# Expert weights in 2 MB transfers, two contraction chunks to a transfer, in a hybrid decoder step on one Trainium2 core

## What is computed

```python
def expert_block(args):
    xb, e = args                       # 128 rows of tokens, the number of an expert
    hgu = xb @ w_gu[e] + b_gu[e]       # w_gu[e]: 1024 x 2048
    gate = jnp.minimum(hgu[:, :D_FF], SWIGLU_LIMIT)
    up = jnp.clip(hgu[:, D_FF:], -SWIGLU_LIMIT, SWIGLU_LIMIT)
    act = (up + 1.0) * gate * jax.nn.sigmoid(SWIGLU_ALPHA * gate)
    return act @ w_down[e] + b_down[e] # w_down[e]: 1024 x 1024
```

## Time and profile before

| | |
|---|---|
| median of 3 runs | 1454.49 us (1453.26 to 1455.03) |
| profiled execution | 1456.36 us, its span 1454.6 us |
| PE busy | 1357.5 us, 93% of the span |
| PE clock granted, whole span | 0.944 |
| DMA moved | 438.82 MB, mean 302 GB/s |
| the 32 blocks of experts | 455.5 us to 1402.2 us |

### The profile page before, as it was taken

One profiled execution on the slowest core, in us unless ns is written; L12 is line 12 of the kernel. 1 busy time (PEld: TensorE's weight loads), 2 busy tenths in 40 slices (PEclk: granted clock), 3 DMA queues, 4 the chain that ended last, 5 costly groups with the idle time before them and its releaser, 6 DMA issues.

```text
span 1454.6 us, 17291 instructions
## 1 busy us (share of the span) xinstructions
PE 1357.5 (93%) x6116; PEld 591.3 (41%) x6116; DVE 506.7 (35%) x1073; ACT 202.2 (14%) x385; POOL 52.4 (4%) x103
## 2 busy tenths in 40 slices
PE   6989995598689999999999999999999999999997
PEld 5765884463443333333333333333333333333332
DVE  2673334525445332233223322232223322332223
ACT  2450010000021111111111111111111111111111
POOL 5100010000020000000000000000000000000000
PEclk8999996687569999999999999999999999999999
DMA  8221104002346999999999999999999999999941
GB/s 253 94 84 58 59 3 176 11 0 83 105 147 247 408 422 422 422 422 422 422 422 422 422 422 422 422 422 422 422 422 422 422 422 422 422 422 422 422 176 36
DMA packets 83620, 438.82 MB, mean 302 GB/s; under 512 B 15114, under 2 KB 22423, under 8 KB 34410
## 3 DMA queue, kind: packets, MB, share of 16 engines
q1 hardware_dynamic: 83594, 438.47, 74.2%
HBM read 433.41 MB, written 5.02 MB: 301 GB/s over the span
## 4 chain that ended last, share of the span: by engine, by line
PE 88%; DVE 6%; issue 1%; DMA 1%; ACT 1%; SPq 1%; POOL 0%; POOLq 0%; DVEq 0%; ACTq 0%
PE bank L936 32%; PE bank L946 15%; PE bank L926 7%; PE bank L900 6%; PE bank L570 5%; PE bank L956 3%; PE bank L696 2%; PE bank L1035 2%; PE bank L568 1%; PE bank L908 1%; DVE SC L1366 1%; PE bank L916 1%; PE bank L648 1%; DMA SC<-in_ple_w 1%; PE bank L841 1%
## 5 line engine op out<-in xcount | busy, mean ns | idle before, releaser
L936 PE MATMUL bank<-ring,SC 128*64 128x512 f32 x2048 | 479.1, 600 | 0.7 <-ACT SC L1225 0.7
L936 PEld LDWEIGHTS bank<-ring,SC 128*64 128x64 f32 x2048 | 133.2, 136 | 282.2 <-issue 277.5
L946 PE MATMUL bank<-ring,SC 128*64 128x512 f32 x1024 | 226.8, 595 | 0.0
L1708 DVE TENSOR_TENSOR SC<-bank,bgu 128x256 f32<-128x256 f32 x128 | 48.1, 418 | 437.1 <-PE bank L956 437.1
L1700 DVE TENSOR_TENSOR X<-X,bank 128x512 f32<-128x512 f32 x180 | 115.2, 680 | 97.1 <-PE bank L926 97.1
L946 PEld LDWEIGHTS bank<-ring,SC 128*64 128x64 f32 x1024 | 70.7, 137 | 133.3 <-issue 133.3
L570 PE MATMUL bank<-xT,ring 128*128 128x320 f32 x384 | 109.3, 440 | 0.0
L926 PE MATMUL bank<-SC 64*128 64x512 f32 x360 | 101.6, 641 | 0.0
L900 PE MATMUL bank<-XS,SC 128*64 128x512 f32 x396 | 90.6, 592 | 0.7 <-ACT va L1211 0.7
L570 PEld LDWEIGHTS bank<-xT,ring 128*128 128x128 f32 x384 | 73.1, 194 | 29.7 <-issue 2.4
L1221 ACT ACTIVATE SC<-bank 128x512 f32<-128x512 f32 x33 | 19.7, 598 | 407.0 <-PE bank L900 407.0
(11 more groups left out here) (415 smaller groups left out, 1066.3 us busy)
## 6 DMA issues: line engine op xcount, KB each, us to landing
ring<-in_expert_w_gu SPq DMA_DIRECT2D x256, 1024.0 KB, 15.7
ring<-in_expert_w_down SPq DMA_DIRECT2D x128, 1024.0 KB, 16.4
ring<-in_w_in SPq DMA_DIRECT2D x7, 2048.0 KB, 8.5
ring<-in_w_out SPq DMA_DIRECT2D x1, 4096.0 KB, 14.6
ring<-in_ple_gate_w SPq DMA_DIRECT2D x4, 1024.0 KB, 12.2
out_gdn_s<-ring SPq DMA_DIRECT2D x1, 2048.0 KB, 8.7
X<-in_x_prompt SPq DMA_DIRECT2D x2, 512.0 KB, 3.8
out_c_s<-ring SPq DMA_DIRECT2D x1, 1024.0 KB, 5.9
```

Source lines behind the costliest of these rows:

```text
L936: last = mm(PB[j][SL * h:SL * h + SL, :], xg[:, c % 4, c // 4, :], w[:, FF * h + 512 * j:FF * h + 512 * j + 512], start=(c == 0), stop=(c ...
L946: last = mm(PB[4][SL * h:SL * h + SL, :], act_t[:, 2 * (c - NGU) + kk, :], w[:, D * kk + 512 * h:D * kk + 512 * h + 512], start=(c == NGU ...
L1708: ins = V.tensor_tensor(out[:, 4 * i:4 * i + 4, :], PB[2 + i][:, :].rearrange("p (k h s) -> p k h s", k=4, h=2)[:, :, h, :], bgu[:, c0 + 4 ...
```

## The change

Every pair of chunks becomes one 2 MB transfer, in which each partition gets 16 KB that lie in one piece in memory: two adjacent rows of gate-and-up (in place of rows 128 apart), four adjacent rows of down (in place of two). SP waits for the second chunk of a pair to be used before it issues the pair; PE waits at the even chunks only, on the semaphore of the pair. To match the new order of rows, `turn_rows` takes every second column of `xrow` (before: adjacent ones), and `turn_hidden` and the turns of the biases take every fourth column (before: every second).

```diff
-        w_gu = a["expert_w_gu"].rearrange("o e (k p) n -> (o e) p k n", p=P)
-        w_dn = a["expert_w_down"].rearrange("o e (j p i) n -> (o e) p j (i n)", p=P, i=2)
+        w_gu = a["expert_w_gu"].rearrange("o e (j p i) n -> (o e) p j (i n)", p=P, i=2)
+        w_dn = a["expert_w_down"].rearrange("o e (j p i) n -> (o e) p j (i n)", p=P, i=4)
...
-        def pair_cols(m):
-            return slice(2 * P * (m // 2) + m % 2, 2 * P * (m // 2 + 1), 2)
-        def load_chunk(eng, e, c):
-            if c < NGU:
-                src, dst = w_gu[e, :, c, :], slot(c)
-            else:
-                src, dst = w_dn[e, :, c - NGU, :], slot(c)
+        def spread(m, n):
+            return slice(n * P * (m // n) + m % n, n * P * (m // n + 1), n)
+        def load_pair(eng, e, c):
+            dst = ring[:, c * SLOTW:(c + 2) * SLOTW]
+            src = w_gu[e, :, c // 2, :] if c < NGU else w_dn[e, :, (c - NGU) // 2, :]
             eng.dma_start(dst, src).then_inc(sem(f"w_full{c}"), 16)
...
-                for c in range(NGU):
-                    sp.wait_ge(sem("w_used"), used(b, c))
-                    load_chunk(sp, e, c)
+                for c in range(0, NGU, 2):
+                    sp.wait_ge(sem("w_used"), used(b, c + 1))
+                    load_pair(sp, e, c)
...
-                last = turn(PB[2][:, NE * c:NE * c + NE], srow[32:64, pair_cols(c)], ident[32:64, 32:64])
+                last = turn(PB[2][:, NE * c:NE * c + NE], srow[32:64, spread(c, 4)], ident[32:64, 32:64])
...
-                    last = turn(PB[7][:, P * j:P * j + P], xrow[:, P * j:P * j + P], ident[:, :])
+                    last = turn(PB[7][:, P * j:P * j + P], xrow[:, spread(j, 2)], ident[:, :])
...
-                pe.wait_ge(sem(f"w_full{c}"), 16 * b + 16)
+                if c % 2 == 0:
+                    pe.wait_ge(sem(f"w_full{c}"), 16 * b + 16)
...
-                pe.wait_ge(sem(f"w_full{at}"), 16 * b + (16 if at == c else 32))
+                if c % 2 == 0:
+                    pe.wait_ge(sem(f"w_full{at}"), 16 * b + (16 if at == c else 32))
...
-                    last = turn(PB[2 + m // 4][:, P * (m % 4):P * (m % 4) + P], hS[:, pair_cols(m)], ident[:, :])
+                    last = turn(PB[2 + m // 4][:, P * (m % 4):P * (m % 4) + P], hS[:, spread(m, 4)], ident[:, :])
```

More of the change, by code:

```diff
@@ L311, in _ @@
             sp.wait_ge(sem("rows_stored"), 32)
-            for c in range(0, 2):
-                load_chunk(sp, 0, c)
+            for c in range(0, 2, 2):
+                load_pair(sp, 0, c)
             sp.wait_ge(sem("Sp_done"), 2)
@@ L323, in _ @@
             sp.wait_ge(sem("wqST_ps"), 1)
-            for c in range(2, 4):
-                load_chunk(sp, 0, c)
+            for c in range(2, 4, 2):
+                load_pair(sp, 0, c)
             sp.wait_ge(sem("Ss_done"), H)
@@ L329, in _ @@
             sp.wait_ge(sem("S_stored"), 16)
-            for c in range(4, 6):
-                load_chunk(sp, 0, c)
+            for c in range(4, 6, 2):
+                load_pair(sp, 0, c)
             sp.wait_ge(sem("qC_ps"), 2)
@@ L343, in _ @@
             sp.wait_ge(sem("C_stored"), 32)
-            for c in range(6, 8):
-                load_chunk(sp, 0, c)
+            for c in range(6, 8, 2):
+                load_pair(sp, 0, c)
             sp.wait_ge(sem("mnew"), 3)
@@ L349, in _ @@
             sp.wait_ge(sem("x1_ps"), 5)
-            for c in range(NGU, NCK):
-                load_chunk(sp, 0, c)
+            for c in range(NGU, NCK, 2):
+                load_pair(sp, 0, c)
             sp.wait_ge(sem("lg_ps"), 3)
             sp.dma_start(bdr, a["expert_b_down"].rearrange("o e n -> (o e) n")).then_inc(sem("bdr_in"), 16)
-            for c in range(NGU):
-                sp.wait_ge(sem("w_used"), used(0, c))
-                load_chunk(sp, 1, c)
+            for c in range(0, NGU, 2):
+                sp.wait_ge(sem("w_used"), used(0, c + 1))
+                load_pair(sp, 1, c)
             sp.wait_ge(sem("routed"), ROUTED["tables"])
@@ L362, in _ @@
                 e = sp.value_load(etab[0:1, bass.ds(b + 1, 1)], min_val=0, max_val=NE - 1)
-                for c in range(NGU):
-                    sp.wait_ge(sem("w_used"), used(b, c))
-                    load_chunk(sp, e, c)
+                for c in range(0, NGU, 2):
+                    sp.wait_ge(sem("w_used"), used(b, c + 1))
+                    load_pair(sp, e, c)
                 e = sp.value_load(etab[0:1, bass.ds(b, 1)], min_val=0, max_val=NE - 1)
-                for c in range(NGU, NCK):
-                    sp.wait_ge(sem("w_used"), used(b, c))
-                    load_chunk(sp, e, c)
+                for c in range(NGU, NCK, 2):
+                    sp.wait_ge(sem("w_used"), used(b, c + 1))
+                    load_pair(sp, e, c)
             e = sp.value_load(etab[0:1, bass.ds(last_b, 1)], min_val=0, max_val=NE - 1)
[L371 to L374, removed]
+            for i in range(0, NDN, 2):
+                sp.wait_ge(sem("w_used"), used(last_b, i + 1))
+                sp.dma_start(ring[:, i * SLOTW:(i + 2) * SLOTW], w_dn[e, :, i // 2, :]).then_inc(sem(f"w_full{i}"), 16)
             w_ple = a["ple_gate_w"].rearrange("o (k p) n -> p (o k) n", p=P)
```

## The result

The changed kernel takes 1458.04 us (median of 16 runs, 1456.75 to 1460.2) against 1454.7 us for the kernel before in the same measurement (16 runs, 1453.26 to 1456.66). The ratio is 1.0022, 95% interval 1.0015 to 1.003: slower by 3.3 us. The prediction was 1485.6 us with a range from 1458 to 1490; it forecast a loss of 31 us, and a tenth of it came. The time lies just inside the range by luck alone: the lower edge was meant for a small step at every fourth column (B), which did not come. The likeliest case (A) did not happen. The mechanism of C did (a stride of four costs what one of two costs), but not its time of 1456.0 to 1457.0 us, since the term that the prediction gave 1.5 us came out at twice that.

A forecast was written before the change was run, and what follows sets the result against it. PE was taken to bound the loop, with DMA 1.2% slower behind it. Added to the median 1454.5 us, 27.9 (turn_hidden) + 1.7 (L518) + 1.5 (turn_rows) = 31.1 gave 1485.6 us, range 1458 to 1490.

The forecast's parts named there:

- B: Rival: turn_hidden's stride of four costs a small step, 0.133 to 0.160 us a turn: 1459.5 to 1466.8 us; chance 0.22.
- A: Likeliest case: turn_hidden's stride of four halves the weight load's rate, 0.218 to 0.240 us a turn: 1482.7 to 1488.6; chance 0.58.
- C: Rival: turn_hidden's stride of four costs what two does: 1456.0 to 1457.0 us, within 0.2%; chance 0.11.
- What bounds the kernel: Expert loop: PE bounds at 29.47 us a block; DMA needs 29.82, living on a stock the loop cannot use up.
- Waits, issues, later issue and earlier need: Weight loop: six fewer PE waits and half the SP issues gain 0; later pairs cost 0, about 1 us otherwise.
- Transfers of 2 MB: Weight transfers: larger ones gain 0 while PE is the bound; 1 MB ones already reach 422 GB/s.
- Turns with a stride, every fourth column: turn_hidden and L518 bias turns: 0.229 us a turn, adding 27.9 us in the loop and 1.7 us at L518.
- turn_rows from adjacent to alternate columns: turn_rows, groups of 4 turns, 33 times: stride of two costs 0.011 us a turn, 1.5 us in all.
- D: Rival: pairs make transfers late and PE waits for weights; 1465.8 us at 1% under 422 GB/s; chance 0.05.
- E: Rival: faster, freed waits or issues bring PE some 3 to 5 us: 1450 to 1451 us; chance 0.04.

The follow-up runs named there:

- e5: Kernel before, with up chunks 1 to 7 leaving out the matmuls of the second half of the hidden columns, to make DMA the bound: 1448.9 us.
- e4: Kernel before, with ACT's PSUM copies ordering the columns of hS so turn_hidden takes adjacent ones: 1450.1 us against 1455.72.
- e10: Kernel before, with down in rows 128 apart (4 KB pieces), turn_hidden and bias turns on adjacent columns: 1460.54 us against 1455.68.
- e2: Changed kernel, with gate-and-up back in the old row order and turn_rows on adjacent columns, 2 MB transfers kept: 1455.69 us against 1455.72.
- e6: Changed kernel (16 KB pieces), with the same up-chunk matmuls left out as in e5: 1436.98 us.
- e7: As e6, but 2 MB transfers with 8 KB pieces, in the row order of the kernel before: 1449.92 us.
- e8: Kernel before, with turn_rows at every fourth column, turn_hidden and bias turns at every eighth, 1 MB transfers: 1455.56 us against 1455.3.
- e9: Kernel before, with only turn_hidden and the bias turns at every eighth column, 1 MB transfers: 1452.77 us against 1455.68.
- e3: Changed kernel, with ACT's PSUM copies ordering the columns of xrow and hS so all turns take adjacent ones: 1452.53 us against 1455.72.

## Why the prediction was wrong

**What bounds the kernel: right.** PE is the bound, DMA follows slightly slower, and its stock lasts through the loop. e5 measures DMA's own 29.82 us a block, the figure worked out ahead; e4 and e10 follow the same arithmetic to where it holds (24 us to landing) and to where it breaks.

**Waits, issues, later issue and earlier need: right.** All at about 0 (e2, loop +0.11 us, which is `turn_hidden`'s).

**Transfers of 2 MB: right that they gain nothing here.** The rate does rise, by the piece of 16 KB and not by the 2 MB (e6 against e7). The page's figures ("DMA: Bandwidth & Descriptors", Measured, of the Trainium skill) tell of the size of a transfer, issued from GpSimd and not from SyncE as here; no difference by that size is seen here between 1 and 2 MB with the queue full.

**Turns with a stride, every fourth column: wrong, and this is the step that failed.** The prediction said that from alternate to every fourth column the load would take about twice as long, 0.229 us a turn, 27.9 us in the loop and 1.7 at L518. The runs showed 0.120 for both: 0.12 us in the loop instead of 27.9, and nothing at L518, where the 13 turns at the end take 1.74 us in the changed kernel as before. The upper end of the estimate took the places read as what the load waits for, already the limit at a stride of two, so that four doubles the time. Four does not (e2), and eight, which by that argument would double it again, is cheaper than both (e8 and e9). What misled was the recorded duration of the load, 209 against 140 ns, taken to say that the load had come out from behind what hid it. The recorded duration does not tell the pace, and the trace of the kernel before had a row that says so: the turns at L516 (of 24 rows) take adjacent columns at 0.11 us each, with a load recorded longer than that of L956,

```profile
L516 PEld LDWEIGHTS bank<-ident,ring x12: 178/219/219, 12.4 to 13.5; 24*128 24x128 f32 x12
```

and in e10 the bias turns, the same shape as at L518 but on adjacent columns, have

```profile
L532 PEld LDWEIGHTS bank<-ident,ring x16: 176/219/219, 14.0 to 15.6; 32*128 32x128 f32 x16
...
14.36 1.57 PE L532 MATMUL bank<-ident,ring 32*128 32x32 f32 x13
```

which is (1.57 - 0.29)/12 = 0.107 us a turn at 219 ns, against 0.120 at 212 ns with alternate columns at L518. Turns counted from start to start had said 0.12 against 0.11 all along. The page that was weighed there ("Advanced Engine Details and Errata", SBUF Cachelines, of the Trainium skill) asks for two accesses to a 16-byte line. For the turns' weight loads the trace does not agree: with two accesses to a line (stride 2) and with one (stride 4) they take the same time, 1.15 and 1.16 us for eight, and with two they already take longer than with adjacent columns.

**turn_rows from adjacent to alternate columns: the mechanism right, the size off by two.** 1.5 us were forecast, 2.9 came. The sum took 0.011 us a turn, the difference in pace. A group of four goes from 0.59 to 0.68, which is 0.04 for four turns' pace and 0.05 more once in each group. The starts of the single turns show both parts: the first step of a group is 0.17 us with adjacent columns, 0.22 at a stride of two or four and 0.21 at eight, and the later ones are 0.109, 0.118 to 0.122 and 0.110 to 0.114. Comparing 8 with 4 turns shows them too: with adjacent columns 1.02 against 0.59, with alternate ones 1.15 against 0.67 or 0.68; the difference for four more is 0.11 and 0.12 each, and what remains for the group is 0.15 and 0.20. The prediction divided a run of 13 turns at the start (of the 16 at L518), from which the first step had dropped out, and used the quotient for groups of 4. Its cross-check, "at most 0.013 a turn" from the groups of 8 and 4, does not come out of those rows: 1.15 - (0.59 + 4 x 0.109) = 0.12 us a group of 8, 0.016 a turn, and a group of 4 pays 0.022 a turn. Why the first step of a group is longer was not tested.

**The rivals.** Of C the mechanism happened, with 2.9 us in place of its 1.5, so that the loss is 0.22% and not within its 0.2%. B did not, nor D (the time to landing fell instead of growing). E did not; that waits on PE were free was borne out.

## What to carry to other kernels

When PE is busy without a gap and DMA's share is 1.01, look at how the time to landing moves through the loop: it tells which of the two bounds the loop, by how much the other is behind, and how many blocks its stock lasts. If it is PE, a longer piece for DMA is worth nothing by itself, and what it costs PE in the order of its operands is paid in every block; that order can be made by an engine with time to spare (here ACT's copies out of PSUM, whose recorded time did not change), and this, not the transfers, gave the gain: e4 has it without them. Price short groups by groups of the same length, from start to start, and do not extrapolate a small step of unknown cause to a doubling.

## What the runs showed of the hardware that was not expected

- The cost of a stride in the stationary operand of a float32 turn does not grow with distance from two to eight: eight turns take 1.02 us with adjacent columns, 1.15 at every second and every fourth, and 1.08 at every eighth (the weight load is recorded as 141, 209, 209 and 193 ns). Why eight is cheaper stays open.
- The recorded duration of a weight load does not tell the pace of the turns: with adjacent columns 140 ns in the loop and 219 at the start, at 0.11 us a turn in both.
- ACT reads every second or every fourth element of PSUM as fast as adjacent ones (597 ns for 128x512, e4 and e3).
- DMA's rate by the length of a partition's piece, 1 or 2 MB transfers and a full queue: 428 GB/s at 16 KB, 422 at 8 KB, 418 with a third of the bytes in 4 KB pieces. Between 1 MB and 2 MB at 8 KB there is no difference, though the number of small packets halves.
